# The order of down products, gate and up products and row transposes in a mixture-of-experts loop on one core

## The reference

```python
for e in range(N_EXPERTS):
    act = jax.nn.silu(hf @ w_gate[e]) * (hf @ w_up[e])
    y = y + combine[:, e:e + 1] * (act @ w_down[e])
...
x = x + gate2 * y
```

## Time and profile before

| | us |
|---|---|
| median of three runs | 1770.94 |
| profiled execution, its time | 1773.78 |
| profiled execution, its span | 1772.0 |
| PE busy with products in the span | 1621.0 (91%) |
| DVE busy | 804.1 (45%) |
| ACT busy | 539.3 (30%) |
| POOL busy | 73.6 (4%) |

### The profile page before, as it was taken

The page is one execution under the profiler, slowest core; times in us unless marked ns, Lnnn a source line. Parts: engine busy times, 40 slices in busy tenths (PEclk is TensorE's granted clock), DMA queues, the critical chain, the costliest instruction groups (busy, mean ns, idle before and its releaser), DMA issues.

```text
span 1772.0 us, 20143 instructions
## 1 busy us (share of the span) xinstructions
PE 1621.0 (91%) x8271; PEld 1209.7 (68%) x8271; DVE 804.1 (45%) x1375; ACT 539.3 (30%) x874; POOL 73.6 (4%) x90
## 2 busy tenths in 40 slices
PE   3999999999996999999998999999999984887775
PEld 3997777777785788888886786797678872333232
DVE  4466343354353657665223863426653524221111
ACT  5234443344432322222113523322353331111010
POOL 3000000000000000000000000000000001211111
PEclk8999999999997999999999999989999996989998
DMA  4333312112324456564222221211214527999993
GB/s 132 107 96 114 101 49 72 59 61 71 91 91 128 132 170 198 170 215 138 96 95 69 72 87 56 72 48 55 65 53 160 215 85 314 401 410 385 404 394 99
DMA packets 146128, 258.33 MB, mean 146 GB/s; under 512 B 16268, under 2 KB 120888, under 8 KB 132720
## 3 DMA queue, kind: packets, MB, share of 16 engines
q1 hardware_dynamic: 138512, 241.44, 38.9%
q0 software_dynamic: 7520, 15.56, 3.1%
HBM read 251.69 MB, written 15.23 MB: 151 GB/s over the span
## 4 chain that ended last, share of the span: by engine, by line
PE 84%; DVE 6%; issue 5%; DMA 2%; ACT 2%; POOL 0%; SPq 0%; POOLq 0%; DVEq 0%; ACTq 0%
PE psum L2284 20%; PE psum L2285 20%; PE psum L2286 20%; PE psum L2852 7%; PE psum L2869 3%; PE psum L2604 1%; PE psum L2593 1%; PE psum L2576 1%; PE psum L2830 1%; DMA Xg<-h_rows,tok 1%; PE psum L2497 1%; DVE WL L1453 1%; PE psum L2349 1%; ACT Sb L1042 1%; PE psum L2517 1%
## 5 line engine op out<-in xcount | busy, mean ns | idle before, releaser
L2284 PE MATMUL psum<-AH,WH 128*128 128x512 f32 (+1 forms) x1240 | 490.8, 396 | 13.7 <-DVE AL L1499 6.3
L2285 PE MATMUL psum<-AL,WH 128*128 128x512 f32 (+1 forms) x1240 | 475.1, 383 | 0.0
L2286 PE MATMUL psum<-AH,WL 128*128 128x512 f32 (+1 forms) x1240 | 472.0, 381 | 0.0
L1453 DVE TENSOR_TENSOR WL<-raw,WH 128x2048 fp32r<-128x2048 f32 (+1 forms) x100 | 226.6, 2266 | 185.1 <-ACT WH L953 184.5
L2284 PEld LDWEIGHTS psum<-AH,WH 128*128 128x128 f32 x1240 | 235.7, 190 | 78.0 <-issue 19.8
L2286 PEld LDWEIGHTS psum<-AH,WL 128*128 128x128 f32 x1240 | 236.3, 191 | 46.3
L2285 PEld LDWEIGHTS psum<-AL,WH 128*128 128x128 f32 x1240 | 236.2, 190 | 43.8 <-issue 3.1
L953 ACT ACTIVATE WH<-raw 128x2048 fp32r<-128x2048 f32 (+1 forms) x100 | 189.0, 1890 | 142.7 <-PE psum L2286 107.5
L2852 PE MATMUL psum<-WE,XT 128*64 128x512 f32 x544 | 131.2, 638 | 23.0 <-issue 21.1
L2852 PEld LDWEIGHTS psum<-WE,XT 128*64 128x64 f32 x544 | 47.9, 147 | 104.3 <-issue 104.3
L2869 PE MATMUL psum<-WE,AT 128*64 128x512 f32 x272 | 64.7, 618 | 28.3 <-issue 26.7
(11 more groups left out here) (503 smaller groups left out, 1958.8 us busy)
## 6 DMA issues: line engine op xcount, KB each, us to landing
raw<-w_in SPq DMA_DIRECT2D x45, 1024.0 KB, 5.2
WE<-w_gate SPq DMA_DIRECT2D x34, 1024.0 KB, 15.5
WE<-w_up SPq DMA_DIRECT2D x34, 1024.0 KB, 30.6
WE<-w_down SPq DMA_DIRECT2D x34, 1024.0 KB, 28.6
araw<-w_ada SPq DMA_DIRECT2D x24, 1024.0 KB, 6.2
raw<-w_ffn_in SPq DMA_DIRECT2D x22, 1024.0 KB, 6.1
raw<-w_ffn_out SPq DMA_DIRECT2D x11, 1024.0 KB, 4.8
raw<-w_out SPq DMA_DIRECT2D x8, 1024.0 KB, 5.1
```

What stands on the lines that cost most here:

```text
L1453: V.tensor_tensor(WL[:, n, 0:w], raw[:, n, 0:w], WH[:, fed[0] % HL, 0:w].bitcast(F32), ALU.subtract).then_inc(S_("lo_ready"), 1)
L2284: MM(dst, lh, rh, start=first, stop=False)
L2285: MM(dst, lh, rl, start=False, stop=False)
L2286: return MM(dst, ll, rh, start=False, stop=last)
```

## The change

Only the order of instructions changes; no instruction is added or taken away, and no buffer or semaphore.

- On the PE, `down(t)` stands behind `gate_up(t+1)` and `transpose_rows(t+2)`, and `transpose_act(t)` opens the round of pair t.
- On DVE, `y_scaled(t-1)` stands behind `gated(t)` and `xt_copy(t+1)`.
- On POOL only the second loop changes, which does not run for these inputs: it issues its gathers two pairs ahead, as the first loop did already.
- ACT and SP are unchanged.

```diff
             with pool.If(more_tiles(pool)):
                 gather(BASE)
+                gather(BASE + 1)
                 for t in range(BASE, NPAIR):
-                    if t + 1 < NPAIR:
-                        gather(t + 1)
+                    if t + 2 < NPAIR:
+                        gather(t + 2)
                     scatter(t)
...
                     gated(t)
                     if t + 1 < t1:
                         xt_copy(t + 1)
-                    y_scaled(t)
+                    if t > t0:
+                        y_scaled(t - 1)
+                y_scaled(t1 - 1)
...
             def pairs(t0, t1):
+
                 transpose_rows(t0)
+                gate_up(t0)
+                if t0 + 1 < t1:
+                    transpose_rows(t0 + 1)
                 for t in range(t0, t1):
-                    gate_up(t)
+                    transpose_act(t)
                     if t + 1 < t1:
-                        transpose_rows(t + 1)
-                    transpose_act(t)
+                        gate_up(t + 1)
+                    if t + 2 < t1:
+                        transpose_rows(t + 2)
                     down(t)
```

## The result

The changed kernel takes 1865.43 us (median of four runs, 1861.46 to 1865.94), the kernel before 1771.27 in the runs beside it: a ratio of 1.0526, 95% interval 1.0508 to 1.0545. The change makes the kernel 94 us slower. The prediction was 1865.0.

The account below looks back on a forecast made before the run. Loads bound the loop before; the closed gather chain would bound it after. Opening to 1511.4, 14 rounds to 1836.4 and a tail of 29.8 gave span 1866.2, on the median 1865.1 us; 8-in-10 range 1828 to 1893.

Parts of the forecast that it names:

- The closed chain: Loop: down products, scaling, scatter, gather, row transposes, down products become the bound; PE waits 8.5 us for each round's gather.
- The gather at 11.4 us: Loop: each gather flies in full load traffic and takes the median 11.4 us to land, range 10.0 to 12.0.
- The clock at 2.2 us per round: Row transposes and down products behind the idle wait: lowered clock adds 2.2 us, making them 6.9 us together.
- Pair 3 at 23.7 us: Pair 3 scatters twice; from the end of its down products to the gather's landing 23.7 us, in place of 15.7.
- The 14 rounds: Pairs 1 to 14, gathers 3 to 16: 13 x 15.7 + 23.7 + 14 x 6.94 us, ending with down(14) at 1836.4.
- The opening: Start of the loop: down(0) now follows gate_up(1) and transpose_rows(2), so y_done of pair 0 comes at 1511.4, before 1503.7.
- The tail: From the end of down(14) to the end of the span: 29.8 us, with the last scatter waiting for pair 15's landing.
- The loads' pause: Opening: SP stands at the downs of pair 3 and loads pause about 3 us, hidden with a round of 22.6 us.
- the first rival: Loop: the loads stay the bound, gathers landing in under 8.7 us; about 1775 us, or 1771 if hidden; chance 0.06.
- faster: Loop: the PE's 1.74 us per pair count and its round falls to 12.0 us; at best 1741 us; chance 0.04.
- Clock up: Loop: the chain closes but the clock stays up; span 1835, median 1834 us; chance 0.12.
- The all-slow end: Loop: row transposes and down products slow throughout (8.19 us) and gathers of 12.0 us; 1890 us; chance 0.12.

Follow-up runs that it names:

- e7_busy_wait_long: Changed kernel with 66 identity transposes on the PE ahead of each transpose_rows(t+2), inside the wait for the gather; 1845.69 us.
- n3_lead_no_loads: Changed kernel with gather(t+3) ahead of scatter(t) on POOL, and without the weight loads of pairs 3 to 16; 1709.61 us.
- e3_busy_wait: Changed kernel with 48 identity transposes on the PE ahead of each transpose_rows(t+2), inside the wait for the gather; 1865.03 us.

## Why the prediction was right

Point by point, with the terms of its sum:

- The closed chain: shown. Every pair from 3 to 16 waits for its gather, 14 waits as foretold, and moving the gathers alone takes 87 us away. No gate and up product waits for loads. Twelve of the waits are 7.9 to 9.4 us, for the 7 to 9 foretold; the one at pair 6 is 12.7, not 16, and the last 4.35. The starts of successive down products are 23.3 us apart in the mean (18.7 to 27.7), for 22 to 23.
- The gather at 11.4 us: those behind a plain scatter, but for the last, twelve in all, took 11.9 in the mean, 5.5 us more in sum. The choice of the loaded figure over the 4.9 was the one that decided: without the loads it is 5.2.
- The clock at 2.2 us per round: row transposes took 1.97 each time and down products 5.2 in the mean, together 7.1 for the 6.9 put in; 2.5 us more in sum. The run e7_busy_wait_long shows that the idle PE is the cause: with it occupied, 1.1 and 3.65 come back. The 2.2 itself mixed two views: 8.78 and 9.29 are from the timeline, where the unslowed products read 7.09, and 6.87 is from the chain of waits. On the timeline alone the extra is 1.9, and the sum would be 3 us smaller.
- Pair 3 at 23.7 us: 20.1 (1576.9 to 1597.0). The gather behind its second scatter landed in 6.1 us, not 10.0; it started at 1590.8, when the burst of loads was nearly through (DMA share 0.95 from 1592 to 1594, 0.24 from there to 1597). 3.6 us less. The last gather likewise, 7.5 us, no more gate and up loads being beside it: 3.9 less.
- The 14 rounds: 325.4 us measured (from the end of `down(0)` at 1505.6 to that of `down(14)` at 1831.0), 325.0 predicted. The four errors cancel to 0.4 us, and with the opening and the tail the loop grew by 93.7 us for the 94.2 predicted. The mechanism was right; that the sum agrees to half a microsecond is luck, since its terms were off by 2.5 to 5.5 us each.
- The opening: from `transpose_rows(0)` to the end of `down(0)` 28.0 us, predicted 27.8. The tail: 28.7, predicted 29.8. The scatter of pair 15 landed in 5.1 us, and the last one waited for it as foretold.
- The loads' pause: it is there (in the changed kernel the DMA share is 0.04 from 1504 to 1506); it costs nothing, no gate and up product waiting for loads. It costs once the chain is opened: that kernel is 6.3 us over the one before (1778.73 against 1772.44), not the 4 of the first rival, and SP's new list gives all of it back.
- The loads as the bound before: right in sum, but the 17.7 us are those of the later rounds only. The gate and up products waited eight times, from pair 9 on, 0.4 to 4.6 us each (rows 3 show three of them); the rounds ahead of that took the PE's 13.7 us, but for the one of pair 6, on weights that were in the slots already.
- The bytes of a gather: the prediction put 512 KB, the trace has some 0.26 MB, and so the 7.3 MB of a round are 6.8. The sum doesn't suffer, since it took the gather's time from rows and not from bytes.
- The rule of two us plus bytes by bandwidth (the Trainium skill, DMA: Bandwidth & Descriptors, section Anatomy of one DMA) gives for the 0.26 MB an estimate of 2.6 us, and not the 3.2 worked out for 512 KB. It is not reached even with the DMAs nearly free: 5.2 is the median there and 4.1 the shortest, most of them with a scatter just ahead in the same queue. The shortest of any run, 3.2 us, is the gather of pair 3 in n3_lead_no_loads, alone on the DMAs and with only 0.07 MB.

The four rivals: loads stay the bound, and faster, are refuted by the time. Clock up is what e7_busy_wait_long made by force, and its 21.1 us per round are near the 20.4 given. The all-slow end did not come; the down products were slow in their first part only, 4.2 to 5.8 us of at most 6.2.

## What to carry to other kernels

Before an instruction is moved back in one engine's list, follow what its result releases on the other engines until the path comes back to the list it started from. Here it came back over DVE and POOL to a gather that the work now ahead of it needed, and a slack of 4.9 us became a wait of 8.7. When the order on one engine changes, look at the lists of the others too (prefetches on POOL, loads on SP, the copy order on DVE); here each of them in the wrong order cost by itself, 87 and 7 us by the ratios, and for DVE 23 in the variant with the down products first. And a wait removed from an engine that is not the bound is worth nothing until the bound moves.

## What was not expected of the hardware

With 2.6 to 4.6 us idle ahead of the row transposes the granted clock was down for them and much of the down products in 8 of 12 rounds, although the PE had done 5.5 us of other work in the same wait (e3_busy_wait). In two rounds with 3.40 us idle the outcome differs: rows of 1.97 us in one and 1.16 in the other. With 0.6 to 2.1 us idle (e7_busy_wait_long) rows and downs were at full speed in all of 12 rounds but one; after the 4.9 us at pair 6 they were slow. So the length of the idle stretch alone doesn't settle it. In the changed kernel without loads, where it was 1.6 to 2.4 us, the down products took 5.35 us in 4 of 13 rounds, behind row transposes at full speed:

```profile
1610.83 1.16 PE L2830 MATMUL psum<-cst,Xg 128*128 128x128 f32 x8 [1.94 <-DMA Xg<-h_rows,tok]
1611.92 5.35 PE L2869 MATMUL psum<-WE,AT 128*64 128x512 f32 x16
```

Why the dense part takes longer in one execution than in another, up to 6 us between the starts of the loop in the profiles of before and after, stays open.
